# First block's modulation rows: four halves at once in TensorE's column tiles, made during the two attentions

## What is computed

```python
# first block, layer l of 2
c_act = silu(c)                                   # (1, 1024)
mod = c_act @ w_ada[l] + b_ada[l]                 # (1, 6144) = six rows of 1024
sh_m, sc_m, gt_m, sh_f, sc_f, gt_f = split(mod, 6)
h = rms_norm(x, g_pre_mix[l]) * (1 + sc_m) + sh_m
y = token_mixer(h, ...)                           # w_in, two attentions of 8 heads, w_out
x = x + gt_m * rms_norm(y, g_post_mix[l])
h = rms_norm(x, g_pre_ffn[l]) * (1 + sc_f) + sh_f
y = conv_glu_ffn(h, ...)                          # w_up_act, w_up_lin, w_down
x = x + gt_f * rms_norm(y, g_post_ffn[l])
# the second block then runs an attention and a "peer" (256 gathered rows a token, u and v) on
# context and latent, an mLSTM layer, and a second peer on the latent
```

## Time and profile before

| | us |
|---|---|
| median of 3 runs (3610.74 to 3615.86) | 3613.68 |
| profiled execution, its own time | 3609.14 |
| its span, first to last instruction | 3607.8 |
| TensorE matmul busy in the span | 2909.2 (81%) |
| VectorE busy | 2291.7 (64%) |
| ScalarE busy | 1138.5 (32%) |
| GpSimd busy | 970.6 (27%) |

### The profile page before, as it was taken

The page is one execution under the profiler, slowest core; times in us unless marked ns, Lnnn a source line. Parts: engine busy times, 40 slices in busy tenths (PEclk is TensorE's granted clock), DMA queues, the critical chain, the costliest instruction groups (busy, mean ns, idle before and its releaser), DMA issues.

```text
span 3607.8 us, 30555 instructions
## 1 busy us (share of the span) xinstructions
PE 2909.2 (81%) x9361; PEld 1544.3 (43%) x9361; DVE 2291.7 (64%) x4831; ACT 1138.5 (32%) x2909; POOL 970.6 (27%) x852
## 2 busy tenths in 40 slices
PE   7778877688989678987778787799789788877776
PEld 2344356266533347834437233343354463322222
DVE  1356548699867758865764999544423459975444
ACT  2012122323222343312542444333322224443333
POOL 1000000222322123323321444344300015443332
PEclk9989987699989779998879999999988899999999
DMA  7756733499979658997765999899952259999997
GB/s 269 274 177 224 240 120 126 182 399 344 368 294 399 248 207 346 417 402 269 300 221 199 388 421 421 353 420 421 421 203 76 67 221 421 421 421 422 421 422 328
DMA packets 214630, 1108.81 MB, mean 307 GB/s; under 512 B 25101, under 2 KB 25473, under 8 KB 116161
## 3 DMA queue, kind: packets, MB, share of 16 engines
q0 software_dynamic: 114864, 818.96, 56.2%
q1 hardware_dynamic: 98752, 287.17, 21.9%
q10 hardware_dynamic: 848, 0.72, 0.1%
HBM read 1105.58 MB, written 1.05 MB: 307 GB/s over the span
## 4 chain that ended last, share of the span: by engine, by line
PE 36%; DMA 29%; DVE 25%; ACT 5%; issue 3%; POOL 1%; SPq 1%; ACTq 0%; DVEq 0%; POOLq 0%
DMA AR<-in_uv,AR 23%; PE PS L820 10%; DVE AR L2270 7%; PE PS L2201 5%; PE PS L2114 3%; PE PS L1156 3%; DMA AR<-in_w_in 2%; PE PS L1628 2%; PE PS L2212 2%; DVE AR L371 1%; PE PS L802 1%; DVE AR L2265 1%; PE PS L2352 1%; PE PS L1143 1%; DMA AR<-in_w_down 1%
## 5 line engine op out<-in xcount | busy, mean ns | idle before, releaser
L2320 POOL DMA_INDIRECT AR<-in_uv,AR x768 | 892.8, 1162 | 1592.9 <-PE PS L2201 647.9
L2270 DVE CUSTOM_DVE_ANT_0 AR<-AR 128x1024 f32<-128x1024 f32 x768 | 937.3, 1222 | 505.0 <-DMA AR<-in_uv,AR 501.5
L2201 PE MATMUL PS<-AR 128*128 128x512 f32 x2048 | 973.6, 624 | 284.5 <-ACT AR L2257 278.4
L2201 PEld LDWEIGHTS PS<-AR 128*128 128x128 f32 x2048 | 388.0, 197 | 863.5 <-ACT AR L2257 446.0
L820 PE MATMUL PS<-AR 128*128 128x512 f32 (+3 forms) x1080 | 465.6, 583 | 32.0 <-DMA AR<-in_w_in 22.0
L2239 ACT ACTIVATE AR<-AR 128x2 f32<-128x2 f32 x384 | 78.1, 203 | 1147.1 <-DVE AR L2270 1143.7
L1143 PE MATMUL PS<-AR 128*128 128x256 f32 x1408 | 327.0, 391 | 14.3 <-DMA AR<-in_w_up_lin 9.6
L820 PEld LDWEIGHTS PS<-AR 128*128 128x128 f32 x1080 | 203.3, 203 | 275.8 <-issue 227.8
L1143 PEld LDWEIGHTS PS<-AR 128*128 128x128 f32 x1408 | 271.3, 195 | 81.9 <-issue 20.3
L2257 ACT ACTIVATE AR<-C,AR 128x128 f32<-128x128 f32 (+1 forms) x614 | 241.0, 392 | 20.1
L371 DVE SCALAR_TENSOR_TENSOR AR<-AR,CC 128x512 f32<-128x512 f32 x252 | 191.6, 760 | 83.1 <-DMA AR<-in_w_ada 39.3
(11 more groups left out here) (240 smaller groups left out, 2677.7 us busy)
## 6 DMA issues: line engine op xcount, KB each, us to landing
AR<-in_w_ada SPq DMA_DIRECT2D x160, 256.0 KB
AR<-in_w_in SPq DMA_DIRECT2D x56, 512.0 KB
AR<-in_w_mod SPq DMA_DIRECT2D x96, 256.0 KB, 4.4
AR<-in_peer_w_q SPq DMA_DIRECT2D x48, 512.0 KB
AR<-in_w_mod SPq DMA_DIRECT2D x45, 512.0 KB, 12.9
AR<-in_w_up_act SPq DMA_DIRECT2D x44, 512.0 KB
AR<-in_w_up_lin SPq DMA_DIRECT2D x44, 512.0 KB
AR<-in_w_down SPq DMA_DIRECT2D x44, 512.0 KB
```

The lines of the kernel that those rows point to most:

```text
L2201: ins = pe.eng.matmul(acc[i][hh], e.dg(x), e.buf(x)[:, 1024 + 512 * hh:1536 + 512 * hh], start=(x == e.on[False][i][0]), stop=(x == e.on[F ...
L2270: v.eng.tensor_tensor_reduce(e.buf(x)[:, 0:1024], e.buf(x)[:, 0:1024], norm2(e).H[e.tiles[x // 128]], 1.0, 0.0, ALU.mult, ALU.add, DT[x // ...
L2320: g.eng.indirect_dma_start(e.buf(x), None, D["uv"][e.l], bass.IndirectOffsetOnAxis(ap=idx_at(x // 16, x % 16, 1), axis=0)).then_inc(*land. ...
```

## The change

`Quads` replaces `Mods` for the first block. A quad is four halves: for each of eight pieces of the contraction, SP loads four 128x512 blocks (one a half) and TensorE multiplies them in its four column tiles, all in one PSUM bank; four bias matmuls end it, ScalarE copies the bank to `MODt[:, 3584:4096]` and a DMA keeps the four rows in `BR`, partitions 112 to 127. Three quads (layer 0's eight halves and the first four of layer 1) are made in the context's queries and the attention of layer 0, from 16 places in `SL`; two (the other eight of layer 1) in the attention of layer 1, from 8 places in `SC`. `KeptAda` then spreads a kept half over 128 partitions with one matmul from 32 partitions of `BR`, two steps for each chunk of w_out, and for rows 1 and 0 of layer 1 in FFN up. The context's first gathers wait for the three quads' last matmuls, since they write over `SL`. POOL's loads of the gains (g_post_mix, g_pre_ffn, g_post_ffn) move with `KeptAda` to w_out.

```diff
+        class Quads:
+            def sp(self, sp):
+                n = len(self.own)
+                for q, (r0, halves) in enumerate(self.quads):
+                    for kc in range(8):
+                        for g, (l, r) in enumerate(halves):
+                            i = self.piece(q, kc, g)
+                            sp.wait_ge(("quad", self.key, i - n) if i >= n else self.guard)
+                            sp.eng.dma_start(self.own[i % n], D["w_ada"][l][r, kc // 2, :, 512 * (kc % 2):512 * (kc % 2) + 512]).then_inc(
...
+            def pe(self, pe):
+                for q, (r0, halves) in enumerate(self.quads):
+                    bk = bank(pe, SIDE, "quad", self.key, q)
+                    for kc in range(8):
+                        for g, (l, r) in enumerate(halves):
+                            pe.wait_ge(("raw", self.key, i))
+                            pe.eng.matmul(bk[32 * g:32 * g + 32, :], CC[:, kc:kc + 1].to_broadcast([128, 32]), self.own[i % n],
+                                          start=(kc == 0), stop=False).then_inc(*pe.done("quad", self.key, i))
+                        if kc == 7:
+                            for g, (l, r) in enumerate(halves):
+                                ins = pe.eng.matmul(bk[32 * g:32 * g + 32, :], ident[0:48, rr:rr + 1].to_broadcast([48, 32]),
+                                                    BR[0:48, :], start=False, stop=True)
+                        yield
+            def keep(self, a, q):
+                a.wait_ge(a.last, ("mm", "quad", self.key, q), ("kept", self.key, q - 1) if q else self.free)
+                a.eng.activation(ROWS_Q, psum("quad", self.key, q), ACT.Copy).then_inc(*a.done("ev", "quad", self.key, q))
+                a.eng.dma_start(BR[r0:r0 + 4, :], ROWS_Q[0:128:32, :]).then_inc(*land.landed("keptq", "kept", self.key, q))
...
+        class KeptAda(KeptMods):
+            def spread_out(self, pe, q):
+                pe.wait_ge(self.made)
+                pe.eng.matmul(bk, ident[96:128, r:r + 1].to_broadcast([32, 128]), BR[96:128, :], start=True,
...
+        def attended(lane, l, steps):
+            for i, _ in enumerate(steps):
+                lane.fill(1 + (i < QUICK[l]), "q")
+                yield ATT[l]
...
         def first_pe(pe, l):
-            pe.run(mods_of["first", l])
-            for i, _ in enumerate(lin_pe(pe, ("win", l), D["w_in"][l], 8, (0, 3656), [0, 1], LAT.tile, prep=n1, ring=FIRST[l],
-                            whole=HEAD[l])):
-                if i >= 4 * len(HEAD[l]):
-                    pe.fill()
-                yield CH
-            pe.flush()
+            for _ in lin_pe(pe, ("win", l), D["w_in"][l], 8, (0, 3656), [0, 1], LAT.tile, prep=n1, ring=FIRST[l], whole=HEAD[l]):
+                yield CH
...
+            pe.run(mods_of["quads", l], "q")
+            pe.fill(1, "q")
...
-            for _ in stages(8, s1, s2, s3):
-                yield ATT[l]
+            yield from attended(pe, l, stages(8, s1, s2, s3))
+            pe.flush("q")
+            pe.run(mods_of["first", l])
...
-                yield CH
+                pe.fill(2)
+                yield CH
+            pe.flush()
             pe.run(mods_of["next", l])
...
-                    g.wait_ge(("idx", e.key, x // 16), ("sum", e.key, b) if b is not None else None)
+                    g.wait_ge(("idx", e.key, x // 16), ("sum", e.key, b) if b is not None else
+                              mods_of["quads", 0].summed() if e.halved else None)
...
             for share in queries(lane, of_ctx):
+                lane.fill(1, "q")
                 yield PACE * share
```

154 lines of the change are left out of this document (105 added, 49 removed).

## The result

The changed kernel takes 3560.3 us (median of 4 runs, 3554.7 to 3565.9) against 3614.1 for the kernel before: 0.985 of its time, interval 0.983 to 0.987, 54 us less. The forecast was 26 us less. The profiled execution took 3554.7 us, 3553.4 of it span.

What follows compares the result with a forecast made beforehand. No engine was taken to bound it throughout: VectorE and DMA fill w_in and FFN up, while the attentions have room. Gains of 83 less costs of 57 took 26 off 3613.7, to 3588 us; range 3560 to 3622.

Steps and rivals of the forecast that it cites:

- the three full stages: w_in of layer 0, FFN up of layer 0 and w_in of layer 1: gains of 28, 24 and 18 us.
- w_out of layer 1: Cost of 12 us (7 to 20): eight spread matmuls, VectorE evictions and a late g_pre_ffn gain load.
- w_in of layer 0: Gain of 28 us (17 to 47) from six halves: TensorE 12, VectorE's sums 7, loads 9.
- flips: Ahead of layer 0's flips: without the last two halves they follow L502, gain of 13 us (8 to 13).
- FFN up: Layer 0: 25 steps at 4.4 instead of 5.6 us, less 6 given back; gain of 24 us.
- at best -32: Largest gain allowed in FFN up of layer 0 by the other engines' floor: DMA 101 us, TensorE 109.
- w_in of layer 1: Gain of 18 us (8 to 28): TensorE's 12 for six halves and about half of 15.5 us of load waits.
- Attentions: Costs of 16 us in layer 0 and 15 in layer 1: matmuls half hidden in idle time, plus waits.
- First gathers and w_out of layer 0: Costs of 4 us for gathers waiting on the third quad and 10 for spread matmuls, evictions and gain loads.
- the full stages stay full: Rival: gains are TensorE's own matmuls and little else, 52 against costs of 57; 3619 us, chance 0.14.
- The tiles do not pay between full matmuls: Rival: column tiles run serially or mode changes cost a full matmul; 3663 us and up, chance 0.02.

Runs made afterwards that it cites:

- b_pe: Kernel before with the two closing matmuls of each of the first block's 20 modulation halves cut to 8 of 512 columns; 3603 us.
- b_two: Kernel before with the first block's modulation sums cut to 8 columns and its loads to 8 partitions, closing matmuls in full; 3570 us.
- b_all: Kernel before with the first block's modulation sums, loads and closing matmuls all still issued but each cut small; 3539 us.
- b_late: Kernel before with the first block's halves in w_in of layer 0 begun two steps later on every engine, nothing left out; 3595 us in one run.
- b_gone: Kernel before with small closing matmuls, one of eight loads a half, and only the first and a small last of its eight sums; 3517 us.
- b_dma: Kernel before with the first block's modulation weight pieces cut to 8 of 128 partitions once every place has been filled; 3612 us.
- b_noload: Kernel before with small sums and closing matmuls, and only the first of a half's eight pieces loaded (20 loads instead of 160); 3537 us.
- a_gains: Changed kernel with POOL issuing the three gain loads of each w_out stage together ahead of the stage; 3562.3 us.
- a_qpe: Changed kernel with the quads' matmuls of groups 2 to 8 cut to 8 of 512 columns, loads and order kept; 3551.7 us in one run.

## Why the prediction was half right

The direction, the side on which each stage moves and the price of a group of column tiles were right; the sum was half of what came. What failed are the gains of the three full stages, put at 28, 24 and 18 us, which came as 44, 36 and 35, and one cost, w_out of layer 1, put at 12, which came as 24. The gains were added up from TensorE's closing matmuls as if each were on the chain, from part of the loads and sums on the chain, and from a pace a step at the old clock. The cuts show in their place two limits that hold the stage together, the number of instructions in each order, and the clock that rises when they go.

- *w_in of layer 0, 28 for 44, and flips 13 for 9.* The term counted TensorE's 12 us, 7 of sums and 9 of loads. By themselves the 12 gave nothing (b_pe begins the queries at 459.7); with the other two cut they gave 11.8 (b_two to b_all), near the spread of this point. It lacked SP's order: a piece whose guard was open only at 85.4 us stood ahead of a main-line load, worth 9 us by b_late. The row that shows it was quoted, 7.62 us of idle time for in_even_w_in, for another purpose. That b_all and b_gone get more than each cut also says that a line's share of the chain, from which the term took its loads and sums, is no bound for what goes with it. The flips gained 9 and not 13 because they do not start where L502 ends: TensorE waits 4.4 us there for VectorE's rotation. TensorE in time, kernel after:

```profile
435.83 1.04 PE L502 MATMUL PS<-BR,C 48*32 48x512 f32 x2
441.31 6.84 PE L754 MATMUL PS<-C,AR 128*128 128x128 f32 x42 [4.44 <-DVE AR L1510]
```

- *FFN up, 24 for 36.* The step that failed is "At 4.4 the 25 take 110 instead of 140 us". The 4.4 us a step was read from the stretch behind 851 us, where VectorE, at 88 of 95 us, was still the limit; the steps after the change take 4.3. And the 6 us that four spread matmuls and a first weight load were to give back did not show, since the clock rose from 0.95 to 0.99 and TensorE's busy time fell by 18 us (200.9 to 183.0) where 8 of work went. The floor given as "at best -32" is the window's 133 us less DMA's 101; TensorE's 109, at the old clock, would by the same sum allow 24. The 25 steps went from 140.1 to 106.4 us, a gain of 34, over both.
- *w_in of layer 1, 18 for 35.* Half of 15.5 us of waits and 12 us of TensorE; in the trace no wait for w_in loads is left among the larger ones, and the clock went from 0.94 to 0.98. b_dma gives 12 for the bytes, b_noload 10 more for the number of loads, which the term did not count; TensorE's 12 give 0.3 by themselves and 6.9 after the other cuts.
- *Attentions, 16 for 20 and 15 for 17.* Right in size. The mechanism was right for bank 7 (6 forecast, 7.5 us waited) and high for the matmuls (13 for 8); 7 of layer 0's 20 are the late gathers, which this term did not have. In layer 1 the waits came as forecast, 3.9 us for the bank and 3.8 for pieces, 3 and 3 forecast. The 40 idle us that its matmuls were to hide in are those of a window of 124 us that reaches 33 us into w_out; the attention itself, 91 us long, has 27. Half of 18 was taken either way.
- *First gathers and w_out of layer 0, 14 for 13.* Right in sum, by luck. The late gathers did not cost their 4 us here, but 7 in the attention; the spread matmuls, eight at 0.95, give back 0.8 when cut; and the wait for the norm, not in the term, grew by 4.0.
- *w_out of layer 1, 12 for 24.* Eight matmuls and a late gain were the whole term. It lacked what stands behind a waiting eviction on VectorE, the norm of the first tile (7.3 us more of TensorE's wait), and the wait for bank 7 (4.9). The late gain, which it had, gives nothing when loaded early (a_gains).

Of the rivals, "the full stages stay full" fell: the gathers keep the DMA share at 0.96, yet the stage is 36 us shorter. "The tiles do not pay between full matmuls" fell too: a group takes 1.06 us. At full clock a group between other matmuls holds TensorE for 1.09 us (1.00 from its start to the next start, and 0.09 by which its own start comes later than that of a further record before it would), two groups in a row take 0.93 each, and a full matmul of 512 columns takes 0.88 (L888 above, eight in 7.06). The rule of the Trainium skill, TensorEngine Tiling (Array Packing), Key Properties, that a change of tiling mode drains the array, costs here at most the 0.2 us between 1.09 and 0.88, in and out together. (The rivals' sums count 43 groups where the terms have 27 + 18 = 45, and give FFN up's matmuls 15 us without a working.) For the clock the trace agrees in direction with the Trainium skill, TensorE: Matmul & The Clock Gate, HAM oscillation, by which idle gaps send it back to its low level: with its gaps filled, attention of layer 0 runs at 0.86 instead of 0.81, and at 0.81 again when a_qpe makes the groups small (its window, 452 to 604):

```profile
452.00:604.00 152.00, 118.03 (x787) 96.52 (x786) 106.22 (x334) 45.90 (x136) 8.75 (x11) 0.81 0.70 248
```

## What to carry to other kernels

When a stage has two engines above nine tenths, take the work off both before judging either: here single cuts of 2 to 7 us became 19 together and 35 with the instructions gone. Read each in-order queue for the first instruction whose wait ends late, and ask what stands behind it; a guard on SP, a copy on ScalarE and a wait for a whole set where a part would do were worth 9, 7 and 7 us, and evictions one step later in w_out of layer 0 some 5. Take more than one profile before a difference of a few us in a stage is read. Price a stage that is relieved at the clock it will have, not at the one it has.

## What was not expected of the hardware

Loads of 8 partitions and sums of 8 columns were far from free in a full stage: 42 such loads, with the waits for them, still cost 4.6 us in FFN up and 10.4 in w_in of layer 1, 36 such sums 8.0 and 1.9. And TensorE's granted clock moved with the stage around it: FFN up ran at 0.96 with one limit cut, 0.98 with two and 1.00 with nothing left. TensorE's busy time fell by 16 us from the first to the last, of which the closing matmuls of six halves, at 2.0 us each in full, are less than 12.
